# A decoder step with a gated-delta layer: the 8x8 diagonal inverses computed on GpSimd by way of DRAM, and joined key products

## What is computed

```python
kb = k * beta[..., None]
lmat = jnp.einsum('nbhcd,nbhed->nbhce', kb, k) * decay_strict
eye = jnp.eye(c, dtype=jnp.float32)
tmat = lax.linalg.triangular_solve(lmat + eye, jnp.broadcast_to(eye, lmat.shape),
                                   left_side=True, lower=True, unit_diagonal=True)
u_base = jnp.einsum('nbhce,nbhef->nbhcf', tmat, v * beta[..., None])
w_dec = jnp.einsum('nbhce,nbhed->nbhcd', tmat, kb * jnp.exp(gc)[..., None])
qk = jnp.einsum('nbhcd,nbhed->nbhce', q, k) * decay_incl
...
def step(s, xs):
    u_b, w_c, qg_c, qk_c, kd_c, gl = xs
    u = u_b - jnp.einsum('bhcd,bhde->bhce', w_c, s)
    o = jnp.einsum('bhcd,bhde->bhce', qg_c, s) + jnp.einsum('bhce,bhef->bhcf', qk_c, u)
    s = s * jnp.exp(gl)[..., None, None] + jnp.einsum('bhcd,bhce->bhde', kd_c, u)
    return s, o
```

## Time and profile before

| | |
|---|---|
| median of 3 runs | 2040.3 us (2038.79 to 2040.34) |
| the profiled execution | 2039.55 us, its span 2037.8 us |
| TensorE clock granted, mean | 0.999 of full |
| share of the span with DMA engines busy, queue of SyncE | 49.1% |
| queue of ScalarE | 0.7% |
| packets, bytes | 380859, 311.13 MB |
| sixteen heads | about 80 to 1040 us of the span |

### The profile page before, as it was taken

The page is one execution under the profiler, slowest core; times in us unless marked ns, Lnnn a source line. Parts: engine busy times, 40 slices in busy tenths (PEclk is TensorE's granted clock), DMA queues, the critical chain, the costliest instruction groups (busy, mean ns, idle before and its releaser), DMA issues.

```text
span 2037.8 us, 51762 instructions
## 1 busy us (share of the span) xinstructions
PE 2018.8 (99%) x19467; PEld 1948.0 (96%) x19467; DVE 1291.1 (63%) x2350; ACT 908.1 (45%) x1940; POOL 163.5 (8%) x355
## 2 busy tenths in 40 slices
PE   9999999999999999999999999999999999999998
PEld 8999999999999999999899999999999999999998
DVE  5877777777777777777755445555546656654443
ACT  6455455455454545545533334333333333433343
POOL 5101101111010110100100000000000000000010
PEclk9999999999999999999999999999999999999999
DMA  8554455555445555445554444544455445544443
GB/s 245 160 151 133 133 160 160 162 150 145 125 142 164 165 151 152 133 131 157 168 180 155 134 161 153 168 146 156 142 159 160 141 146 162 161 157 136 158 134 111
DMA packets 380859, 311.13 MB, mean 153 GB/s; under 512 B 19993, under 2 KB 377066, under 8 KB 380522
## 3 DMA queue, kind: packets, MB, share of 16 engines
q1 hardware_dynamic: 378648, 305.74, 49.1%
q10 hardware_dynamic: 2146, 4.52, 0.7%
HBM read 283.85 MB, written 27.25 MB: 153 GB/s over the span
## 4 chain that ended last, share of the span: by engine, by line
PE 96%; DVE 1%; DMA 1%; ACT 1%; issue 0%; SPq 0%; DVEq 0%; ACTq 0%
PE ps L300 29%; PE ps L301 27%; PE ps L302 27%; PE ps L1259 9%; PE ps L1423 2%; DMA wraw<-in_delta_w_in_dram 1%; PE ps L1409 0%; DMA xtok<-in_x_sample_dram 0%; PE ps L1394 0%; ACT xhi L604 0%; DVE wlo L287 0%; PE ps L1804 0%; PE ps L1397 0%; PE ps L2069 0%; PE ps L2093 0%
## 5 line engine op out<-in xcount | busy, mean ns | idle before, releaser
L300 PE MATMUL ps<-xhi,whi 128*128 128x320 f32 x3072 | 982.3, 320 | 5.6 <-DVE xlo L1035 2.0
L302 PE MATMUL ps<-xhi,wlo 128*128 128x320 f32 x3072 | 949.0, 309 | 0.0
L301 PE MATMUL ps<-xlo,whi 128*128 128x320 f32 x3072 | 948.6, 309 | 0.0
L287 DVE TENSOR_TENSOR wlo<-wraw,whi 128x1024 fp32r<-128x1024 f32 x480 | 576.1, 1222 | 169.6 <-ACT whi L282 167.1
L282 ACT ACTIVATE whi<-wraw 128x1024 fp32r<-128x1024 f32 x480 | 496.6, 1055 | 290.9 <-PE ps L302 272.4
L300 PEld LDWEIGHTS ps<-xhi,whi 128*128 128x128 f32 x3072 | 576.8, 188 | 30.2 <-issue 20.4
L301 PEld LDWEIGHTS ps<-xlo,whi 128*128 128x128 f32 x3072 | 577.4, 188 | 0.9
L302 PEld LDWEIGHTS ps<-xhi,wlo 128*128 128x128 f32 x3072 | 576.7, 188 | 0.0
L300 PE MATMUL ps<-bhi,whi 128*128 128x320 f32 x512 | 157.7, 308 | 0.0
L301 PE MATMUL ps<-blo,whi 128*128 128x320 f32 x512 | 157.6, 308 | 0.0
L302 PE MATMUL ps<-bhi,wlo 128*128 128x320 f32 x512 | 157.6, 308 | 0.0
(11 more groups left out here) (352 smaller groups left out, 2028.8 us busy)
## 6 DMA issues: line engine op xcount, KB each, us to landing
wraw<-in_delta_w_in_dram SPq DMA_DIRECT2D x384, 256.0 KB, 3.0
wraw<-in_pool_w_in_dram SPq DMA_DIRECT2D x256, 256.0 KB, 3.1
wraw<-in_delta_w_out_dram SPq DMA_DIRECT2D x128, 256.0 KB, 3.3
wraw<-in_pool_w_out_dram SPq DMA_DIRECT2D x128, 256.0 KB, 3.2
s_s<-in_state_delta_dram SPq DMA_DIRECT2D x32, 512.0 KB, 6.4
out_dram<-s_s SPq DMA_DIRECT2D x32, 512.0 KB, 4.2
wraw<-in_pool_w_group_dram SPq DMA_DIRECT2D x64, 256.0 KB, 3.1
dec<-gc_rows SPq DMA_DIRECT2D x16, 320.0 KB, 4.1
```

What stands on the lines that cost most here:

```text
L287: nc.vector.tensor_tensor(wlo[:, slot, :], wraw[:, slot, :], whi[:, slot, :].bitcast(F32), ALU.subtract).then_inc(E("w_lo"), 1)
L300: mm(o, whi[:, slot, w], hi[:, k_x, :], start=first, stop=False)
L301: mm(o, whi[:, slot, w], lo[:, k_x, :], start=False, stop=False)
L302: done = mm(o, wlo[:, slot, w], hi[:, k_x, :], start=False, stop=last)
```

## The change

- Levels 1 and 2 on TensorE are gone, for all units, with x0 and its copies. The loop over levels begins at LEVEL_8 = 3, and only for the four large units.
- ScalarE writes lmat (five units of 128x128, 320 KB) to a DRAM buffer, l_blocks. It reads the 80 diagonal 8x8 blocks back, one to a partition (n8, 8 rows of 32 bytes a partition).
- GpSimd computes the inverses of the 8x8 blocks in place by substitution: 12 tensor operations in a row, each waiting for the last, and a memset of the diagonal.
- ScalarE writes them to a second buffer, x_blocks, which was filled with zeros once, and reads the diagonal 32x32 blocks from it in four DMAs into xc. VectorE transposes xc into yc (y2).
- The tiles are dealt anew: 24 ahead of level 3 instead of 17, 2 and 1 in each level after; both passes over the states stand ahead of level 3, and wait for a_t.
- ScalarE scales eight states ahead of level 3 and eight in it. splits 4, 5 and 6 are ahead of level 3.
- The three products of keys with keys and the three of keys with queries become three of keys with both, 256 columns each, in D2 and D3.
- GpSimd's `decay_hidden` for the next head stands behind its new work.

```diff
...
+    UNIT = P * P + P
+    l_dram = nc.dram_tensor("l_blocks", (5 * UNIT,), F32, kind="Internal").ap()
+    x_dram = nc.dram_tensor("x_blocks", (5 * UNIT,), F32, kind="Internal").ap()
+    def unit_rows(t):
+        return t.rearrange("(u y) -> u y", u=5)[:, 0:P * P].rearrange("u (p c) -> p u c", c=P)
+    def small_blocks(t):
+        return t.rearrange("(b x) -> b x", x=8 * P + 8)[:, 0:8 * P].rearrange("b (r w) -> b r w", w=P)[:, :, 0:8]
+    def strip_blocks(t, h):
+        at = h * (BL * P + BL)
+        return t.rearrange("(u y) -> u y", u=5)[:, at:at + BL * P].rearrange("u (s w) -> s u w", w=P)[:, :, 0:BL]
...
@@ -569,6 +585,20 @@
...
+            x8 = n8[0:80, :].rearrange("p (r c) -> p r c", c=8)
+            pool.wait_ge(E("m_in"), n * 16)
+            for m in range(1, 7):
+                if m > 1:
+                    pool.wait_ge(E("x8"), n * 13 - 14 + 2 * m)
+                prod = t8[0:80, 0:(7 - m) * m].rearrange("p (r c) -> p r c", c=m)
+                gp.tensor_tensor(prod, x8[:, m + 1:8, m:m + 1].to_broadcast([80, 7 - m, m]),
+                                 x8[:, m:m + 1, 0:m].to_broadcast([80, 7 - m, m]), ALU.mult).then_inc(E("x8"), 1)
+                if m == 1:
+                    gp.memset(n8[0:80, 0:64:9], 1.0).then_inc(E("x8"), 1)
+                pool.wait_ge(E("x8"), n * 13 - 13 + 2 * m)
+                gp.tensor_tensor(x8[:, m + 1:8, 0:m], x8[:, m + 1:8, 0:m], prod, ALU.add).then_inc(E("x8"), 1)
 
             next_hidden()
...
             decays_turned(n)
+            act.wait_ge(E("l_mat"), n)
+            act.dma_start(unit_rows(l_dram), lmat[:]).then_inc(E("m_out"), 16)
             split(3)
+            act.wait_ge(E("m_out"), n * 16)
+            act.dma_start(n8[0:80, :].rearrange("p (r c) -> p r c", c=8), small_blocks(l_dram)).then_inc(E("m_in"), 16)
...
+            def scaled(first, last):
+                for q in range(first, last):
+                    done = sc.activation(s_s[:, q // 2, q % 2, :], s_s[:, q // 2, q % 2, :], ACT.Copy,
+                                         scale=cur[:, EGL + 4 + q:EGL + 5 + q])
+                return done
             split(4)
-            for k in range(1, TILE_LEVELS + 1):
-                units = 5 if k < S_LEVELS else 4
+            split(5)
+            act.wait_ge(E("x8"), n * 13)
+            act.dma_start(small_blocks(x_dram), n8[0:80, :].rearrange("p (r c) -> p r c", c=8)).then_inc(E("x_out"), 16)
+            act.wait_ge(E("x_out"), n * 16 + 16)
+            for h in range(4):
+                act.dma_start(xc[BL * h:BL * h + BL, :, :], strip_blocks(x_dram, h)).then_inc(E("x_in"), 16)
+            split(6)
+            act.wait_ge(E("ksqs_ps"), n)
+            scaled(0, 8)
+            for k in range(LEVEL_8, TILE_LEVELS + 1):
                 if k == TILE_LEVELS:
                     act.wait_ge(E("lp5"), n)
                     sc.activation(p5[:], blocks(D0[:, 0:P], 4), ACT.Copy).then_inc(E("p5"), 1)
                     split(8)
...
+                act.wait_ge(E("lxt"), n * 3 - 5 + k)
+                if k < TILE_LEVELS:
...
-                if k < 4:
-                    split(4 + k)
-                if k == 2:
-                    act.wait_ge(E("ksqs_ps"), n)
-                if k in (2, 3):
-                    for q in range(6) if k == 2 else range(6, 16):
-                        last = sc.activation(s_s[:, q // 2, q % 2, :], s_s[:, q // 2, q % 2, :], ACT.Copy,
-                                             scale=cur[:, EGL + 4 + q:EGL + 5 + q])
-                if k == 3:
-                    last.then_inc(E("s_scaled"), 1)
+                if k == LEVEL_8:
+                    split(7)
+                    scaled(8, 16).then_inc(E("s_scaled"), 1)
...
@@ -824,6 +863,9 @@
...
         sc.activation(small[:, 61:62], ones[:, 0:1], ACT.Copy).then_inc(E("act_round"), 1)
+        act.wait_ge(E("consts"), 65)
+        act.dma_start(unit_rows(x_dram), ym[:]).then_inc(E("x_out"), 16)
+        act.wait_ge(E("x_out"), 16)
...
             for u in range(5):
-                last = v.scalar_tensor_tensor(lmat[:, u, :], D3[:, P * (u % 2 if u < 4 else 2):P * (u % 2 if u < 4 else 2) + P],
-                                              nb[:, u:u + 1], dec[:, u, :], ALU.mult, ALU.mult)
+                kk = D2[:, 256 * (u % 2) + P:256 * (u % 2) + 256] if u < 4 else D3[:, P:256]
+                last = v.scalar_tensor_tensor(lmat[:, u, :], kk, nb[:, u:u + 1], dec[:, u, :], ALU.mult, ALU.mult)
             last.then_inc(E("l_mat"), 1)
-            dve.wait_ge(E("c_all"), 1)
-            dve.wait_ge(E("l_mat"), n)
-            for h in range(4):
-                r = slice(BL * h, BL * h + BL)
-                last = v.copy_predicated(x0[r, :, :], level[r, 0:1, :].to_broadcast([BL, 5, BL]), lmat[r, :, BL * h:BL * h + BL])
-            last.then_inc(E("x0"), 1)
-            dve.wait_ge(E("x0"), n)
-            v.transpose(yc[:], x0[:]).then_inc(E("y0"), 1)
...
-            dve.wait_ge(E("qk_ps"), n)
             dve.wait_ge(E("dec_t"), n)
             for q in range(2):
-                v.tensor_tensor(a_t[:, 2 * q:2 * q + 2, :], blocks(D2[:, 0:256], 2), dec_t[:, 2 * q:2 * q + 2, :], ALU.mult)
-            v.tensor_tensor(a_t[:, 4, :], D2[:, 256:384], dec_t[:, 4, :], ALU.mult).then_inc(E("at"), 1)
+                v.tensor_tensor(a_t[:, 2 * q:2 * q + 2, :], blocks(D2, 2)[:, :, 0:P], dec_t[:, 2 * q:2 * q + 2, :], ALU.mult)
+            v.tensor_tensor(a_t[:, 4, :], D3[:, 0:P], dec_t[:, 4, :], ALU.mult).then_inc(E("at"), 1)
...
             split(3)
             qk_next()
-            for k in range(1, TILE_LEVELS + 1):
-                units = 5 if k < S_LEVELS else 4
+            split(4)
+            conv_next(0, 0)
+            conv_next(0, 1)
+            split(5)
+            conv_next(0, 2)
+            dve.wait_ge(E("x_in"), n * 64)
+            v.transpose(yc[:], xc[:]).then_inc(E("y2"), 1)
+            conv_next(0, 3)
+            for k in range(LEVEL_8, TILE_LEVELS + 1):
+                units = 4
...
-                    conv_next(0, k - 1)
...
+            qk_t = (silu[:, 0:2, 0:P], silu[:, 0:2, P:2 * P], samp[:, 0:2, :])
...
             for u in range(3):
-                last = one(D3[:, P * u:P * u + P], k_t[u], k_t[u])
+                last = one(blocks(D2[:, 256 * u:256 * u + 256] if u < 2 else D3[:, 0:256], 2), k_t[u], qk_t[u])
             last.then_inc(E("kk_ps"), 1)
-            for u in range(3):
-                last = one(D2[:, P * u:P * u + P], k_t[u], q_t[u])
-            last.then_inc(E("qk_ps"), 1)
...
                 if part == 0:
+                    pe.wait_ge(E("at"), n)
                     pe.wait_ge(E("kq_m"), n)
                     pe.wait_ge(E("state_landed"), n * 32)
...
-            fill(17 - first)
-            for k in range(1, TILE_LEVELS + 1):
-                units = 5 if k < S_LEVELS else 4
+            fill(24 - first)
+            for part in range(2):
+                states_part(part)
+            for k in range(LEVEL_8, TILE_LEVELS + 1):
+                units = 4
 
                 pe.wait_ge(E("ident"), 1)
                 pe.wait_ge(E(f"y{k - 1}"), n)
...
-                fill((3, 2, 3, 3, 2)[k - 1])
-                x = x0 if k == 1 else xc
+                fill(2)
                 pe.wait_ge(E("ident"), 1)
                 if k == TILE_LEVELS:
                     pe.wait_ge(E("x4"), n)
                 pe.wait_ge(E(f"p{k}"), n)
...
-                if k < 3:
-                    states_part(k - 1)
-                elif k < TILE_LEVELS:
+                if k < TILE_LEVELS:
                     fill(1)
...
```

More of the change, by code:

```diff
@@ L41 @@
 BL = 32
-S_LEVELS = 3
+LEVEL_8 = 3
 PK = 4
@@ L143, in build @@
     kq_m = place(a, "kq_m", [4 * P + 32])
-    x0 = place(a, "x0", [5, BL])
+    n8 = place(a, "n8", [64])
+    t8 = place(a, "t8", [16])
     pc = place(a, "pc", [TILE_LEVELS - 1, 5, BL])
@@ L525, in delta_pool @@
             unit = ident[r, BL * h:BL * h + BL].rearrange("p (o c) -> p o c", o=1)
-            gp.tensor_copy(x0[r, :, :], unit.to_broadcast([BL, 5, BL])).then_inc(E("consts"), 1)
-            pool.wait_ge(E("consts"), 66 + 2 * h)
             gp.tensor_copy(pc[r, :, :, :].rearrange("p k u c -> p (k u) c"), unit.to_broadcast([BL, 20, BL])).then_inc(E("consts"), 1)
-            pool.wait_ge(E("consts"), 67 + 2 * h)
+            pool.wait_ge(E("consts"), 66 + h)
         def decay_hidden(i):
@@ L752, in delta @@
                     split(8)
-                act.wait_ge(E("lxt"), (n - 1) * 5 + k)
-                if k == 1:
-                    sc.activation(yc[:], blocks(D1[:, 0:160], 5), ACT.Copy).then_inc(E("y1"), 1)
-                elif k < TILE_LEVELS:
-                    sc.activation(half_blocks(yc[:, 0:units, :], k, 1), packed(D1, units, k), ACT.Copy).then_inc(E(f"y{k}"), 1)
+                act.wait_ge(E("lxt"), n * 3 - 5 + k)
+                if k < TILE_LEVELS:
+                    sc.activation(half_blocks(yc[:, 0:4, :], k, 1), packed(D1, 4, k), ACT.Copy).then_inc(E(f"y{k}"), 1)
```

(12 more changed lines are left out.)

## The result

The changed kernel took 2100.9 us (median; 2099.7 to 2102.5), the kernel before 2040.3 us beside it. The ratio is 1.030 (95% interval 1.029 to 1.031): slower by 61 us, where 2004.5 was forecast. The forecast of faster was wrong, and the range missed.

A forecast was written before the change was run, and what follows sets the result against it. TensorE, busy 99% of the span, was taken as the bound. 2039.55 us, less 36.1 for removed levels, plus 0.7 for joined products, with no wait, gave 2004.2, stated as 2004.5; range 2000 to 2040, chance 0.80.

The forecast's parts named there:

- What TensorE loses: TensorE's stops for the inverse's levels: three shrink to one of 2.59 us, saving 2.26 us a head, 36.1 in all.
- below 2000 nothing is to be had: Whole kernel: a time under 2000 us would need more than the 39 us the removed work could give.
- the joined products: TensorE's key products, three of 256 columns for six of 128: cost +0.05 us a head, +0.7 us in all.
- The start of the chain: ScalarE starts writing lmat at 386.1 in the sixth head, once lmat is ready and ScalarE has ended dec_t.
- level 4: ScalarE's split and eight scalings after y3, 2.4 us against TensorE's 3.8: y4 not late, bounds 0 to 0.5 a head.
- The write-back: Chain leg after GpSimd: inverted 8x8 blocks, 20 KB in 32-byte rows, to DRAM in 2.0 us (1.5 to 4.2).
- the strips: Last DMA leg of the chain: four reads of the diagonal 32x32 blocks, 3.9 us (2.9 to 5.5).
- lmat to DRAM, 320 KB: First chain leg, ScalarE's write: 3.1 us, in proportion between 2.0 for 128 KB and 4.2 for 512 KB.
- I take 2.5: Second chain leg, reading the 8x8 blocks back, 20 KB in 640 rows of 32 bytes: 2.5 us (1.5 to 4.1).
- GpSimd: ... 3.6: Chain leg of twelve dependent GpSimd operations at 0.29 us plus a memset: 3.6 us, upper end 7.5.
- the margin of 0.6: Before level 3: y2 ready at 401.9, TensorE wants it at 402.5, so no wait, by 0.6 us.
- Rival 2: DMAs of 32-byte rows are slow: chain 3.8 us longer, wait 3.2 us a head, 2055 us; chance 0.15.

The follow-up runs named there:

- e1: Changed kernel without the DRAM chain and GpSimd's block, so the 8x8 inverses are not computed: 1998.3 us, ratio 0.980 to the kernel before.
- e2: Kernel before the change with only the key products joined, three of 256 columns for six of 128: 2040.5 us, ratio 1.000.
- e11: Changed kernel, states loaded after the whole chain, their passes behind level 5, VectorE quiet until GpSimd finishes: 2023.2 us, ratio 0.991 to the kernel before.
- e4: Changed kernel with the sample states' loads moved behind the load of the next head's decays: 2073.2 us, ratio 1.017 to the kernel before.
- e5: Changed kernel with VectorE's splits and convolution pieces held until GpSimd finishes the 8x8 inverses: 2091.1 us, ratio 1.025 to the kernel before.
- e10: Changed kernel with states' loads behind the decays, VectorE quiet until GpSimd finishes, two convolution pieces moved later: 2076.1 us, ratio 1.018 to the kernel before.
- e3: Changed kernel with 28 unused matmuls a head added where TensorE waits for y2: 2072.8 us, ratio 1.016 to the kernel before.
- e6: Changed kernel writing only lmat's diagonal 32x32 blocks, four DMAs of 20 KB for one of 320 KB: 2111.6 us, ratio 1.035 to the kernel before.

## Why the prediction was wrong

- **What TensorE loses: right, and a little low.** 2.26 us a head was forecast, and 40.7 / 16 = 2.54 came (e1), so "below 2000 nothing is to be had" was not so: e1 took 1998.3. The stop that is left is 2.46 instead of 2.59, and the joined products gave 0.15 us a head in the timeline, where a cost of 0.05 was forecast (e2: neither can be measured).
- **The start of the chain: right,** 3.3 us for 3.4. So was the statement that VectorE's changes, the first split and level 4 cost nothing: ahead of y4, ScalarE still idled 0.57 us, and TensorE shows no wait for it. The write-back (2.0) and the strips (3.2 for 3.9) came out too, but by the luck of their place: between 421 and 425 us the DMA share was 0.15. Beside weights the strips' leg was 4.0 us (e11), and beside the states the write-back's was 5.3 (e4).
- **The step that failed first** is "lmat to DRAM, 320 KB: ... in proportion 3.1", and "I take 2.5" for the read. They came to 6.0 and 3.8 us, the first of them over its upper bound of 4.2. The landings of the earlier trace rows were medians from other moments of the step, all but the 40 KB on SyncE's queue; a landing on ScalarE's queue beside a megabyte of states on top of the weights was none of them. What had to be read was SyncE's timeline where the new DMAs would stand, and what is in flight there. The trace of the kernel before had it, in head six and in its DMA issues:

```profile
381.58 1.01 SPq L363 DMA_DIRECT2D s_s<-in_state_delta_dram  x2
382.91 9.70 SPq L270 DMA_DIRECT2D wraw<-in_delta_w_in_dram  x6
```

```profile
s_s<-in_state_delta_dram SPq DMA_DIRECT2D x32, 512.0 KB, 6.4
```

The 4.2 us that served as the upper bound is a store of 512 KB. The load of the same states took 6.4, and issued at 381.58 it was still in flight at 386.1, where the forecast puts lmat's write. Free of the states, the two legs take 2.6 and 2.9 us (e11), and the forecast is right to half a microsecond. By the Trainium skill ("DMA: Bandwidth & Descriptors", section "Anatomy of one DMA"), whose rule is for GpSimd's path, the two would take 2.75 and 2.05 us, as an estimate; e11's 2.6 agrees with the first, its 2.9 is over the second, and that section does not speak of a backlog.
- **The second** is "GpSimd: ... 3.6". The pitch of 0.29 us was read in a moment in which VectorE did nothing with two operands. The upper end of 7.5 us was in the text, from the rows that show such a doubling, but it was not asked what the doubling came from. 1.6 us more.
- **The sum:** 2.9 + 1.3 + 1.6, less 0.8 for the strips (3.15 for 3.9) and 0.2 for the hand-overs, is 4.8 us late, less the margin of 0.6 is 4.2; the wait was 4.03 us in this head, 67.8 in all.
- **The term that was missing:** the clock. Nowhere did the sum or a rival price what TensorE loses after a wait. Head six paid 2.1 us more. By the spans of the profiled executions, over e1's 1996.9 us, a microsecond of this wait cost 1.5 us in the changed kernel and in e5, and 1.6 in e4 and e10 (waits of 3 to 4 us a head). In e11 it cost 1.2, and there TensorE ran at full speed behind head six's 0.52 us. Rival 2's point from which it decides, "a wait of 2.2 us", was too high if the 1.5 holds there, which no run shows: 40.7 us are then gone at 40.7 / 16 / 1.5 = 1.7 us a head.
- **The rivals.** Slower had 0.15, by rows of 32 bytes. The sign was right and the mechanism wrong: e11 has the same rows and lands them in 1.8 us. With a margin of 0.6 us on four legs, none seen in the trace, and GpSimd's upper end, 7.5 for 3.6, that alone made a wait of 3.3 us, 0.82 for faster was too sure.

## What to carry to other kernels

A chain through DRAM has to be laid against the DMA issues of all queues at the place where it will run; a transfer's landing time taken from another place can be half of what it will be, or less. Where a new wait of 3 or 4 us on TensorE is possible, price it at one and a half times its length, as here, if the engine drops to 1.2 GHz behind it, and see whether something can run in it. The idea was sound: with a megabyte of loads and the passes that need them moved behind the chain, VectorE quiet beside GpSimd and one more tile ahead, the same change gives 1.4% in place of costing 3%.

## What was not expected of the hardware

- After 4.03 us of waiting the granted clock was 0.50 in the window of 427 to 430 us, and 28 useless matmuls a head, 69 us of work, made the kernel 28 us faster (e3).
- 20 KB on ScalarE's queue landed in 1.8 us away from the states and in 5.1 to 5.9 us beside their 1 MB on SyncE's (e11, e4, e10), and each of four DMAs of 20 KB in 3.8 (e6), where one of 320 KB took 5.7 (the changed kernel).
- A GpSimd operation of 12 elements took 1.06 us instead of 0.20 beside one operation of VectorE, and its twelve 5.1 instead of 3.4.
